# A three-layer transformer block on one core: the adaptive-modulation vectors in wider pieces, with 32x32 transposes on VectorE in place of full transposes on TensorE

## The reference, cut to what matters

```
def hybrid_layer(x, c, w_mod, b_mod, ...):
    mod = jax.nn.silu(c) @ w_mod + b_mod          # [1,1024] @ [1024,3072]
    shift, scale, gate = jnp.split(mod[:, None, :], 3, axis=-1)
    h = rms_norm(x, g_pre) * (1 + scale) + shift
    ...
    return x + gate * rms_norm(out, g_post)

def second_block(x, c, w_ada, b_ada, ...):
    c_act = jax.nn.silu(c)
    for l in range(2):
        mod = (c_act @ w_ada[l] + b_ada[l])[:, None, :]   # [1,1024] @ [1024,9216]
        sh0, sc0, g0, sh1, sc1, g1, sh2, sc2, g2 = jnp.split(mod, 9, axis=-1)
        h = _rmsnorm(x, norm_g[l, 0]) * (1.0 + sc0) + sh0
        x = x + 0.5 * g0 * _swiglu(h, ffn_w_gate[l, 0], ffn_w_up[l, 0], ffn_w_down[l, 0])
        ...
```

## Time and profile before

| | |
|---|---|
| median of 3 runs | 2701.72 us (2701.53 to 2701.74) |
| the profiled execution | 2700.64 us, its span 2699.3 us |
| TensorE (PE) busy, records of matmuls | 2668.5 us, 99%, 14437 |
| VectorE (DVE) busy | 1624.8 us, 60%, 3251 instructions |
| ScalarE (ACT) busy | 1028.0 us, 38% |
| DMA, mean share of the 16 engines | 39.0% for the main queue, 344820 packets, 327.77 MB |

### The profile page before, as it was taken

How to read it: one execution, slowest core, us unless ns; L and a number is a source line. 1 busy time by engine, 2 the same in 40 slices (tenths; PEclk the granted TensorE clock), 3 DMA queues, 4 the chain that set the end, 5 groups by cost and what they waited for, 6 DMA issues and landing times.

```text
span 2699.3 us, 35105 instructions
## 1 busy us (share of the span) xinstructions
PE 2668.5 (99%) x14437; PEld 2194.2 (81%) x14437; DVE 1624.8 (60%) x3251; ACT 1028.0 (38%) x1773; POOL 15.1 (1%) x43
## 2 busy tenths in 40 slices
PE   8999999999999999999999999999999999999999
PEld 5788888889888888766888889888889666888888
DVE  7766556356776546677876746763336777633334
ACT  4642332435222234665422224322234665422223
POOL 1000000000000000000000000000000000000000
PEclk9999999999999999999999999999999999999999
DMA  8255334133655323511555524542324411223332
GB/s 254 86 174 170 111 98 120 64 107 112 198 189 192 123 94 109 151 32 32 187 187 187 187 90 144 188 140 94 103 85 130 130 63 32 78 95 94 103 96 67
DMA packets 345352, 330.56 MB, mean 122 GB/s; under 512 B 13410, under 2 KB 334694, under 8 KB 345192
## 3 DMA queue, kind: packets, MB, share of 16 engines
q1 hardware_dynamic: 344820, 327.77, 39.0%
q10 hardware_dynamic: 372, 0.55, 0.1%
HBM read 319.89 MB, written 2.10 MB: 119 GB/s over the span
## 4 chain that ended last, share of the span: by engine, by line
PE 93%; DVE 4%; ACT 1%; DMA 0%; SPq 0%; issue 0%; DVEq 0%
PE bank L538 26%; PE bank L540 26%; PE bank L539 26%; PE bank L592 3%; PE bank L2413 1%; PE bank L2442 1%; PE bank L566 1%; PE bank L567 1%; PE bank L568 1%; PE bank L1396 1%; PE bank L1386 1%; DVE w_lo L506 1%; PE bank L2053 1%; DMA mw<-in_w_mod 0%; DVE E L2537 0%; PE bank L2228 0%
## 5 line engine op out<-in xcount | busy, mean ns | idle before, releaser
L538 PE MATMUL bank<-h_lo,w_hi 128*128 128x512 f32 (+1 forms) x2432 | 917.3, 377 | 3.6 <-DVE h_lo L717 2.2
L540 PE MATMUL bank<-h_hi,w_lo 128*128 128x512 f32 (+1 forms) x2432 | 894.2, 368 | 0.0
L539 PE MATMUL bank<-h_hi,w_hi 128*128 128x512 f32 (+1 forms) x2432 | 892.3, 367 | 0.0
L506 DVE TENSOR_TENSOR w_lo<-raw,w_hi 128x1024 fp32r<-128x1024 f32 (+1 forms) x420 | 489.1, 1201 | 324.4 <-ACT w_hi L500 324.2
L500 ACT ACTIVATE w_hi<-raw 128x1024 fp32r<-128x1024 f32 (+1 forms) x420 | 419.7, 1035 | 345.6 <-PE bank L540 322.4
L538 PEld LDWEIGHTS bank<-h_lo,w_hi 128*128 128x128 f32 x2432 | 458.4, 188 | 87.3 <-issue 8.5
L539 PEld LDWEIGHTS bank<-h_hi,w_hi 128*128 128x128 f32 x2432 | 458.8, 189 | 76.4 <-issue 4.9
L540 PEld LDWEIGHTS bank<-h_hi,w_lo 128*128 128x128 f32 x2432 | 457.6, 188 | 77.1
L538 PE MATMUL bank<-a_lo,w_hi 128*128 128x512 f32 (+1 forms) x1056 | 390.9, 370 | 0.0
L540 PE MATMUL bank<-a_hi,w_lo 128*128 128x512 f32 (+1 forms) x1056 | 384.5, 364 | 0.0
L539 PE MATMUL bank<-a_hi,w_hi 128*128 128x512 f32 (+1 forms) x1056 | 384.1, 364 | 0.0
(11 more groups left out here) (322 smaller groups left out, 2554.8 us busy)
## 6 DMA issues: line engine op xcount, KB each, us to landing
swf<-in_w_ada SPq DMA_DIRECT2D x60, 1024.0 KB, 7.9
raw<-in_ffn_w_gate SPq DMA_DIRECT2D x44, 1024.0 KB, 5.4
raw<-in_ffn_w_up SPq DMA_DIRECT2D x44, 1024.0 KB, 5.4
raw<-in_w_in SPq DMA_DIRECT2D x40, 1024.0 KB, 5.1
raw<-in_ffn_w_down SPq DMA_DIRECT2D x32, 1024.0 KB, 5.2
raw<-in_w_in SPq DMA_DIRECT2D x32, 512.0 KB, 5.1
raw<-in_ffn_w_down SPq DMA_DIRECT2D x16, 768.0 KB, 4.5
mw<-in_w_mod SPq DMA_DIRECT2D x8, 1024.0 KB, 11.8
```

What stands on the lines that cost most here:

```text
L506: nc.vector.tensor_tensor(o, r, half(w_his[place_of[i]], i, h)[0].bitcast(F32), ALU.subtract).then_inc(*w_lo.up((i, h)))
L538: nc.tensor.matmul(o, w1, al, start=start, stop=False)
L539: nc.tensor.matmul(o, w1, ah, start=False, stop=False)
L540: return nc.tensor.matmul(o, w2, ah, start=False, stop=stop)
```

## The change

The pieces of the feed-forward stages become 512 columns wide and are loaded and accumulated in two halves of the rows (`sp_wide`, `dve_wide`): half the rows with one unit, the other half with the next, through four buffers `swf` of 8 KB a partition instead of three. So each stage has as many loads of 1 MB as before, at the same places, and half as many accumulations of twice the width. The pieces of the first block keep their widths.

After the last block of rows, VectorE itself transposes the accumulator in blocks of 32x32 into a new tile `flip`, and reduces each block along the free dimension into 4 (8, 16) columns of a new tile `qpart` (`dve_flip`). Each partition then holds the sum over the 32 partitions of its own group. Once per stage PE multiplies all of `qpart` by a new constant `qsum` (one where row and column agree modulo 32), which sums the four groups (`pe_mods`), and VectorE adds the bias for 32 partitions at a time while it takes the columns apart (`dve_mods`). `pe_ada` and `dve_mod` are gone, with all their transposes, PSUM banks and reductions. The constants' second load grows from 1032 to 1160 columns, and all buffers behind `nacc` lie 2816 bytes further on.

```diff
-    return {"b": b1, ("f", 0, 0): ada(0, 1) + ada(0, 2), ("f", 0, 1): ada(1, 0) + ada(1, 1), ("f", 1, 0): ada(1, 2),
+    return {"b": b1, ("f", 0, 0): ada(0, 1, 512) + ada(0, 2, 512),
+            ("f", 0, 1): ada(1, 0, 512) + ada(1, 1, 512), ("f", 1, 0): ada(1, 2, 512),
             ("f", 1, 1): []}
...
+    c["qsum"] = (p[:, None] % 32 == p[None, :] % 32).astype(np.float32)
...
+    flip, qpart = sb("flip", 512), sb("qpart", 192)
...
@@ def dve_ada(n):
         if j >= 4:
-            dve.wait_ge(pe, ("ada", n - 4))
+            dve.wait_ge(dve, ("flip", n - 4))
...
+        dve_flip(n)
+
+    def dve_flip(n):
         wd = ada[n][4]
-        t = bank(("ada", n), ring)
-        pe.wait_ge(dve, ("acc", n))
-        for i in range(0, wd, 128):
-            m = turn(t[:, i:i + 128], ada_acc(n)[:, i:i + 128])
-        m.then_inc(*pe.up(("ada", n)))
-
-    def dve_mod(n):
-        st, j, w, c0, wd, m = ada[n]
-        q, k = c0 // 128, wd // 128
-        d = mod[m][:, q:q + k]
-        dve.wait_ge(pe, ("ada", n))
-        nc.vector.tensor_reduce(d, ps.of(("ada", n))[:, 0:wd].rearrange("p (m n) -> p m n", m=k), AX, ALU.add).then_inc(
-            *dve.up(("mod0", n), lets=("ada", n)))
         dve.wait_ge(dve, PREV)
-        bias = V(f"b_ada{m - 1}" if m else "b_mod")
-        nc.vector.tensor_tensor(d, d, bias[:, q:q + k], ALU.add).then_inc(*dve.up(("mod", n)))
+        nc.vector.transpose(flip[:, 0:wd], ada_acc(n)).then_inc(*dve.up(("flip", n)))
+        dve.wait_ge(dve, PREV)
+        q = ada_at(n)
+        nc.vector.tensor_reduce(qpart[:, q:q + wd // 32], flip[:, 0:wd].rearrange("p (m n) -> p m n", n=32), AX,
+                                ALU.add).then_inc(*dve.up(("part", n)))
+
+    def sp_wide(n, hf):
+        st, j, w, c0, wd, _ = ada[n]
+        i = wide_slot(n, hf)
+        if j >= 2:
+            sp.wait_ge(dve, ("acc", n - 2, 4 * hf + 3))
+        elif st != ("f", 0, 0):
+            sp.wait_ge(dve, ("acc", n - j - 1, 7))
+        nc.sync.dma_start(view(swf[i], 4, wd), wview(w, c0, wd, 4 * hf, 4)).then_inc(*wide_in[i].up((n, hf), 16))
+
+    def dve_wide(n, hf):
...
+        for a in range(4):
+            k = 4 * hf + a
...
+            dve.wait_ge(dve, ("acc", n, k - 1))
+            nc.vector.scalar_tensor_tensor(acc, v[:, a, :], cv[:, k:k + 1], acc, ALU.mult, ALU.add).then_inc(
+                *dve.up(("acc", n, k)))
+        if hf:
+            dve_flip(n)
+
+    def pe_mods(st, ring):
...
+        pe.wait_ge(dve, ("part", ada_end[st]))
+        n = ada_cols(st)
+        nc.tensor.matmul(t[:, 0:n], cst["qsum"], qpart[:, 0:n], start=True, stop=True).then_inc(*pe.up(("mods", st)))
+
+    def dve_mods(st):
+        dve.wait_ge(pe, ("mods", st))
...
+            for r in range(4):
+                r_ = slice(r * 32, r * 32 + 32)
...
+                nc.vector.tensor_tensor(mod[m][r_, q:q + k], ps.of(("mods", st))[r_, o:o + 4 * k].rearrange(
+                    "p (m f) -> p m f", f=4)[:, :, r], bias[r_, q:q + k], ALU.add).then_inc(
...
@@ def pe_ffn(st):
-            if 0 <= n - 2 < len(plan[st]):
-                pe_ada(first + n - 2, F_AUX)
+            if plan[st] and n == 2 * len(plan[st]) + 1:
+                pe_mods(st, F_AUX)
@@ def dve_ffn(st):
-            if n < len(plan[st]):
-                dve_ada(first + n)
+            if n < 2 * len(plan[st]):
+                dve_wide(first + n // 2, n % 2)
...
-            if 0 <= n - 3 < len(plan[st]):
-                dve_mod(first + n - 3)
+            if plan[st] and n == 2 * len(plan[st]) + 2:
+                dve_mods(st)
```

More of the change, by code:

```diff
@@ L79, in host_constants @@
             "k_da": np.concatenate([cd, sd], 1).astype(np.float32)}
-RES = ["ident", "ones", "bones", "tril", "C", "R64", "ca", "any", "quad"]
+RES = ["ident", "ones", "bones", "tril", "C", "R64", "ca", "any", "quad", "qsum"]
 RESW = {"C": 512, "any": 4, "quad": 4}
@@ L603, in build @@
     swb = [sb(f"swb{i}", 1024, at=at_a + 4096 + 16384 * i) for i in range(2)]
-    swf = [sb(f"swf{i}", 2048, at=at_swf + 8192 * i) for i in range(3)]
+    swf = [sb(f"swf{i}", 2048, at=at_swf + 8192 * i) for i in range(4)]
+    wide_in = [sig(f"wide{i}_in") for i in range(4)]
     acc4 = [nacc[:, 0:256], nacc[:, 256:512], rstd[:, 0:256], rstd[:, 256:512]]
-    acc4f = [nacc[:, 0:256], nacc[:, 256:512], tmp[4][:, 0:256], tmp[4][:, 256:512]]
     def ada_slot(n):
[L610 to L613, removed]
+        j = ada[n][1]
+        return (j % 3, swa[j % 3]) if j < 8 else (j % 2, swb[j % 2])
     def ada_acc(n):
         st, j, _, _, wd, _ = ada[n]
-        return (acc4 if st == "b" else acc4f)[j % 4][:, 0:wd]
+        return acc4[j % 4][:, 0:wd] if st == "b" else (nacc, tmp[4])[j % 2][:, :]
     def sp_ada(n):
@@ new lines, in wide_slot @@
+    def wide_slot(n, hf):
+        return (2 * ada[n][1] + hf) % 4
+    def sp_wide(n, hf):
[7 more added lines that the diff above has]
+    def dve_wide(n, hf):
+        acc = ada_acc(n)
+        i = wide_slot(n, hf)
+        v, cv = view(swf[i], 4, 512), csil[:, 8:16]
+        dve.wait_ge(wide_in[i], (n, hf))
+        for a in range(4):
+            k = 4 * hf + a
+            if k == 0:
+                if ada[n][1] >= 2:
+                    dve.wait_ge(dve, ("flip", n - 2))
+                nc.vector.tensor_scalar(acc, v[:, 0, :], cv[:, 0:1], None, ALU.mult).then_inc(*dve.up(("acc", n, 0)))
+                continue
+            dve.wait_ge(dve, ("acc", n, k - 1))
[3 more added lines that the diff above has]
+            dve_flip(n)
@@ new lines, in ada_at, with ada_cols @@
+    def ada_at(n):
+        st = ada[n][0]
+        return sum(a[4] for a in ada[:n] if a[0] == st) // 32
+    def ada_cols(st):
+        return ada_at(ada_end[st]) + ada[ada_end[st]][4] // 32
+    def pe_mods(st, ring):
+        t = bank(("mods", st), ring)
+        pe.wait_ge(dve, ("part", ada_end[st]))
[3 more added lines that the diff above has]
+        dve.wait_ge(pe, ("mods", st))
+        spans, last = [], None
+        for n, (s_, _, _, c0, wd, m) in enumerate(ada):
+            if s_ == st:
+                if m == last:
+                    spans[-1][3] += wd // 128
+                else:
+                    spans.append([m, c0 // 128, ada_at(n), wd // 128])
+                last = m
+        for i, (m, q, o, k) in enumerate(spans):
+            bias = V(f"b_ada{m - 1}" if m else "b_mod")
+            for r in range(4):
+                r_ = slice(r * 32, r * 32 + 32)
+                end = i == len(spans) - 1 and r == 3
+                nc.vector.tensor_tensor(mod[m][r_, q:q + k], ps.of(("mods", st))[r_, o:o + 4 * k].rearrange(
+                    "p (m f) -> p m f", f=4)[:, :, r], bias[r_, q:q + k], ALU.add).then_inc(
+                        *dve.up(("mod", st) if end else ("mod", st, i, r), lets=("mods", st) if end else None))
@@ L1229, in pe_recurrent, with pe_b_mods, dve_b_mods @@
                     dense(name, [(key, bank(key, B_DENSE))], u, m * 128, H, NK)
[L1230 to L1240, removed]
+    def pe_b_mods(s):
+        if s == B_WHEN[-1] + 2:
+            pe_mods("b", A_AUX)
+    def dve_b_mods(s):
+        if s == B_WHEN[-1] + 3:
+            dve_mods("b")
     def dve_b_ada(s):
@@ L1569, in pe_attention @@
                     dense(name, [(key, t)], u, m * 128, H, NK, hook=hook)
-            pe_b_ada(s, A_AUX)
+            pe_b_mods(s)
     def act_attention():
@@ L1622, in dve_attention @@
                 att = dve_att(j)
-            dve_b_mod(s)
+            dve_b_mods(s)
             for m in range(4 if name[0] == "pa" else 2):
@@ L1848, in pe_ffn @@
     def pe_ffn(st):
-        first = ada_no.get((st, 0), 0)
         for n, name in ffn_units(st):
@@ L1907, in act_ffn @@
                 if q == 0 and plan[st]:
-                    act.wait_ge(pe, ("ada", ada_end[st]))
+                    act.wait_ge(dve, ("flip", ada_end[st]))
                 if q < 2:
@@ L1970, in sp_ffn @@
             for j in ([0, 1] if n == 0 else [n + 1]):
-                if j < len(plan[st]):
+                if j < 2 * len(plan[st]):
                     if j == 0:
@@ L1976, in sp_ffn @@
                             sp.wait_ge(pe, ended(("o2", b4[1], 1)))
-                    sp_ada(first + j)
+                    sp_wide(first + j // 2, j % 2)
     ld_da, ld_l2, ld_lam, ld_w2 = sig("da_in"), sig("l2_in"), sig("lam_in"), sig("w2_in")
```

6 lines of the change are left out of this document (2 added, 4 removed).

## The result

The changed kernel takes 2686.17 us, median of 5 runs (2684.80 to 2688.24), against 2701.53 us for the kernel before (5 runs, 2699.78 to 2701.74): ratio 0.9945, 95% interval 0.9933 to 0.9956. The forecast was 2687.2 us, between 2682 and 2691, with 94% on faster. The profiled execution has a span of 2683.5 us, 15.8 less than before's.

A forecast was written before the change was run, and what follows sets the result against it. The prediction took PE's issue queue in the feed-forward stages as the bound, with DVE covered. Its terms, -16.7 + 1.1 - 0.9 + 2.0 = -14.5 us, gave 2686.1 against the profiled execution, 2687.2 us for the runs' median, range 2682 to 2691.

The forecast's parts named there:

- (a): Feed-forward stages and first block: 152 transposes leave PE, at 0.11 us each, 16.7 us less.
- (b): Four plain fp32 matmuls of qsum against qpart added to PE: 1.1 us more, bounds 1.0 and 1.7.
- (c): At 240.99 us, PE's wait for DVE's reduction to free a PSUM bank goes: 0.9 us less.
- (d): Near 228 us, DVE 1.35 us later lengthens PE's wait for outin, 0.66 not won: 2.0 us back, bounds 0 to 4.8.
- (e): Feed-forward stages: wider pieces save about 50 us of DVE work, which buys nothing because PE waits there for nobody.
- (h): Loads: 60 DMAs of 1 MB as before, constants' load 64 KB larger where nobody waits: zero.
- (f): Bias additions at step 27 of the attention and in three stages: zero, 0.5 us kept for the high end.
- (g): Attention, 128-column pieces: reduction and addition swapped for transpose and reduction, zero; 2.4 us if the transpose costs four times.
- the first (each record's 271 ns): PE is held for each removed transpose's whole record, 41.2 us for 152, giving 2662.7 us; chance 3%.
- the second (waits at unit boundaries): Feed-forward stages: PE waits for w_lo at the next unit, 13.2 us brings nothing, giving 2700.4 us; chance 4%.
- the third (a slow transpose): Feed-forward stages: a 512-column DVE transpose at 9.7 us makes PE's weights late, 20.7 us more, 2707.9 us; chance 2%.

The follow-up runs named there:

- narrow_flip: The changed kernel with feed-forward pieces of 256 columns, one a unit, each with its own 32x32 transpose and reduction on VectorE: 2686.69 us.
- turns_twice: The kernel before with each pair of transposes of the feed-forward stages issued twice, 120 more on TensorE: 2712.62 us (1.0045).
- before_late2: The kernel before with one VectorE reduction, ahead of the products near 226 us, issued two times more: 2701.21 us (1.0001).
- after_again: The changed kernel run once more, nothing changed: 2686.80 us in one execution.
- late5_again: before_late5 run once more, nothing changed against it: 2705.45 us in one execution.
- before_late5: The kernel before with one VectorE reduction, ahead of the products near 226 us, issued five times more: 2703.92 us (1.0009).

## Why the prediction was right, point by point

The direction, the place and the mechanism held. By its own steps, with what the trace shows for each:

- (a) was too small. 16.7 us were forecast; the 60 pairs gave 0.27 each, 16.3, and the 24 pieces of the first block some 4.1, together 20.4. The price was read off three steps across the border with a plain step taken as 0.23 instead of 0.227 (0.22 for 0.23), and the next ten steps, each 0.004 to 0.005 too long, were not looked at.
- (b) 1.1 us forecast; in the changed kernel's trace a product of 192 columns moved the matmuls behind it by 0.38, that of 96 columns by 0.25, so some 1.3 for four.
- (c) held: 0.90 gone.
- (d) held as far as it went. DVE was forecast 1.35 us later at outin. It last waits for PE at 216.74 before and 216.29 now, and outin starts at 227.97 and 228.84: 1.32 later. The wait came out at 2.45, inside the 1.7 to 2.5 named. The transpose of 256 columns took 0.45 where 0.485 was taken, and 256 more columns took 0.71 - 0.45 = 0.26 us, 1.0 ns a column. The one element per cycle and lane that the Trainium skill states (Vector Engine (DVE) Microarchitecture Reference, section on the reshape front-end) agrees with a time that grows by the column; the length of a cycle stands in no trace here. What failed is the step from the wait to its price: the clock behind it, 1.7 us, was not thought of, although the same happens in the first 30 us of before's trace after waits of 2.2 and 3.6 us.
- (e) and (h) held: nobody waits for VectorE or a load in the feed-forward stages, and narrow_flip shows that the saving on VectorE buys nothing. The busy time fell by 29.8 us and not by 50. The records of the instructions that make the vectors add up to 344.8 us before and 307.9 now. In the feed-forward stages they fell by 43, not by 50, since (e) counted the hand-overs between passes, which busy time does not hold; the first block's instructions grew by 6.0, which no term counted. Busy time fell by less than the 36.9 that remain because it counts overlapping records once. It changed nothing in the time.
- (f) held: no wait of PE names the bias additions. (g) was put at zero and cost 0.4: one wait of 1.13 became 1.52, since a transpose and a reduction of 128 columns (0.31 and 0.29, with their hand-overs) replace 0.28 and 0.16.

The sum: -14.5, less 3.7 in (a), plus 0.2 in (b), 1.7 for the clock and 0.4 in (g), is -15.9, and the spans differ by 15.8. Errors of 3.7 us one way and 2.3 the other cancelled to within 1.4. That was luck: the forecast, 1.0 us off, was better than its working.

Of the rivals, the first (each record's 271 ns) is refuted by turns_twice, the second (waits at unit boundaries) by the windows, and the third (a slow transpose) by 0.71 us where 9.3 were needed.

## What to carry to other kernels

Where PE is busy without a gap, count what leaves its queue by the distance of starts, and measure that over a whole unit, not over the border alone. Work put on an engine with room to spare is free only where the busy engine never waits for it: the same edit gained 15.3 us in the stages without waits and 0.6 in the first block, where at one place two pieces stood ahead of a product that PE needed. Moving one of them by three steps gained 4.5 us more.

## What the runs showed of the hardware

- A wait of PE of 2.45 to 2.70 us after continuous work is followed by 3.4 or 6.8 us at a granted clock of 0.50 (six profiles of six), one of 1.31 us or less at this place by none. 3.4 us of it cost 1.7 when they lie fully behind the wait. At the start of before_late2 a wait of 3.70 us was followed by none.
- In the mixers, where PE waits about 1.07 us twice within some 18 us, a stretch of 3.4 us at half clock comes in some executions of a kernel and not in others. Near 2182 us the changed kernel's profile has none and that of after_again, the same program, has one, which costs 1.5 us; near 1177 late5_again has one and before_late5 none. Such stretches can be part of what the runs of one kernel differ by, 2 to 5 us here. The windows, after and then after_again:

```profile
2182.00:2186.00 4.00, 3.84 (x29) 2.85 (x28) 3.06 (x12) 1.78 (x7) 0.00 (x0) 1.00 0.00 0
...
2182.00:2186.00 4.00, 4.00 (x20) 3.15 (x20) 1.60 (x5) 0.12 (x1) 0.00 (x0) 0.57 0.00 0
```

- A pair of 128x128 transposes between dense matmuls costs 0.27 us, a second pair behind it 0.20; their records would make 0.54 of a pair.
- A 32x32 transpose on VectorE of 128, 256 and 512 fp32 columns takes 0.31, 0.45 and 0.71 us.
